# The last stage of a hybrid diffusion step: where its rows wait and how its roots are taken

## What is computed

```python
# x: residual stream after the mixer, (1152, 1024); g2: gate row of the context or of the latents
y = moe(hn2, ...)            # 64 experts, 8 for each token, and a shared one
x = x + g2 * y
def rmsnorm(x, g):
    xf = x.astype(jnp.float32)
    y = xf * lax.rsqrt(jnp.mean(xf * xf, axis=-1, keepdims=True) + EPS)
    return (y * g.astype(jnp.float32)).astype(x.dtype)
y_prompt, y_sample = rmsnorm(xp, norm_final), rmsnorm(xs, norm_final)
```

## Time and profile before

| | us |
|---|---|
| median of 3 runs | 2541.48 (2539.81 to 2545.29) |
| the profiled execution, its whole time | 2549.39 |
| its span, first to last instruction | 2547.6 |
| PE busy in the span | 2070.8 (81%) |
| DVE busy in the span | 1286.5 (50%) |
| ACT / POOL busy in the span | 1012.6 / 720.8 |

### The profile page before, as it was taken

How to read it: one execution, slowest core, us unless ns; L and a number is a source line. 1 busy time by engine, 2 the same in 40 slices (tenths; PEclk the granted TensorE clock), 3 DMA queues, 4 the chain that set the end, 5 groups by cost and what they waited for, 6 DMA issues and landing times. The chain is left out here.

```text
span 2547.6 us, 30701 instructions
## 1 busy us (share of the span) xinstructions
PE 2070.8 (81%) x8155; PEld 1358.9 (53%) x8156; DVE 1286.5 (50%) x2145; ACT 1012.6 (40%) x1458; POOL 720.8 (28%) x648
## 2 busy tenths in 40 slices
PE   2786988599867768970999999999999999999950
PEld 0232433346766754440667666667666666666730
DVE  1546443300254563883555545555555555555647
ACT  0334343100111220110666556566666555555631
POOL 4010010000000000444234544443445444544430
PEclk8788999799978888985999999999999999999975
DMA  9322120110000007222996998877888999997454
GB/s 259 121 74 69 66 100 0 59 45 20 23 3 1 1 7 287 76 75 81 333 297 176 312 344 250 291 206 198 247 247 256 301 305 298 313 293 204 105 148 173
DMA packets 114241, 424.52 MB, mean 167 GB/s; under 512 B 22933, under 2 KB 37269, under 8 KB 89229
## 3 DMA queue, kind: packets, MB, share of 16 engines
q1 hardware_dynamic: 62508, 261.05, 27.8%
q0 software_dynamic: 51376, 162.80, 25.4%
q10 hardware_dynamic: 304, 0.02, 0.0%
HBM read 338.68 MB, written 85.66 MB: 167 GB/s over the span
## 5 line engine op out<-in xcount | busy, mean ns | idle before, releaser
L1715 DVE TENSOR_TENSOR wupl<-w,wuph 128x2048 fp32r<-128x2048 f32 x232 | 521.3, 2289 | 547.3 <-ACT wuph L1681 547.3
L1681 ACT ACTIVATE wuph<-w 128x2048 fp32r x232 | 432.0, 1916 | 38.8 <-SPq L1511 36.5
L1632 PE MATMUL bank<-w,hT 128*128 x912 | 416.0, 599 | 0.9 <-issue 0.3
L1614 PE MATMUL bank<-wuph,xTh 128*128 128x512 f32 x920 | 369.9, 402 | 20.2 <-DVE xTl L1724 19.9
L1614 PE MATMUL bank<-wuph,xTl 128*128 128x512 f32 x920 | 361.4, 393 | 0.0
L1614 PE MATMUL bank<-wupl,xTh 128*128 128x512 f32 x920 | 360.5, 392 | 0.0
L1632 PEld LDWEIGHTS bank<-w,hT 128*128 128x128 f32 x912 | 165.6, 192 | 170.9 <-issue 170.8
L1566 POOL DMA_INDIRECT xg<-hn_scratch,idx_g x118 | 212.1, 1798 | 96.0 <-POOL idx_g L1558 93.1
L1574 POOL DMA_INDIRECT yacc_scratch<-y,idx_s x114 | 185.2, 1624 | 114.8 <-ACT y L1672 67.0
L1671 ACT ACTIVATE y<-bank 128x512 f32<-128x512 f32 x114 | 68.2, 598 | 358.1 <-POOLq L1571 203.7
L1614 PEld LDWEIGHTS bank<-wuph,xTh 128*128 128x128 f32 x920 | 174.2, 189 | 58.7 <-issue 25.1
(11 more groups left out here) (319 smaller groups left out, 2624.7 us busy)
## 6 DMA issues: line engine op xcount, KB each, us to landing
w<-in_exp_w SPq DMA_DIRECT2D x192, 1024.0 KB
wada<-in_w_ada POOLq DMA_DIRECT2D x16, 1024.0 KB, 5.9
wg<-in_w_in SPq DMA_DIRECT2D x12, 1024.0 KB, 5.5
x<-x_scratch SPq DMA_DIRECT2D x18, 512.0 KB, 4.1
wada<-in_w_ada SPq DMA_DIRECT2D x4, 2048.0 KB, 22.5
yacc_scratch<-zero POOLq DMA_DIRECT2D x10, 512.0 KB, 9.1
x_scratch<-x SPq DMA_DIRECT2D x9, 512.0 KB
hn_scratch<-hn SPq DMA_DIRECT2D x9, 512.0 KB
```

Of the source, the lines that this page charges most:

```text
L1614: mm = pe.matmul(b_up[j][:, :], x[:, k, :], w[:, :, k, :], start=(k == 0 and i == 0), stop=(k == KT - 1 and i == 2))
L1632: mm = pe.matmul(b_down[half][:, :], hT[:, i, :], w2[:, bass.ds(slot, 1), i, half * 512:(half + 1) * 512].rearrange("p s n -> p (s n)"), s ...
L1681: act.activation(part13(wup[j][0], half), raw13(e % WSLOT, half), ACT.Copy).then_inc(w_high, 1)
L1715: dve.tensor_tensor(part13(wup[j][1], half), raw13(e % WSLOT, half), part13(wup[j][0], half).bitcast(F32), ALU.subtract).then_inc(w_low, 1)
```

## The change

`w13` is allocated in the program instead of in the expert stage. A view of it, `m.late`, cuts its 12,288 floats into twelve rows of 1024. SP's stream in the expert stage ends with a wait for the last low part, and behind it twelve loads into this view: nine residual tiles, two gate rows and the norm row. The last stage has its nine `y` tiles in nine buffers of their own, which SP requests in a row without a wait; `x`, gates and norm row are read where they lie. Stores free no buffer any more. Roots are taken for three tiles by one set of 16 operations on three columns.

```diff
@@ stage_experts
-        w13 = sb("w13", [P, WSLOT, 2, KT, DE])
+        w13 = m.w13
...
                 down_landed(e, e // WSLOT + 1)
+            sp.wait_ge(w_low, pairs(sp) * 4 + 4)
+            for t in range(NT):
+                sp.dma_start(m.late[:, t, :], m.x2[t * P:(t + 1) * P, :]).then_inc(m.s_late, 16)
+            for s in range(2):
+                sp.dma_start(m.late[:, NT + s, :], m.mods[s:s + 1, 5 * D:6 * D].to_broadcast([P, D])).then_inc(m.s_late, 16)
+            sp.dma_start(m.late[:, NT + 2, :], a["norm_final"].unsqueeze(0).to_broadcast([P, D])).then_inc(m.s_late, 16)
@@ stage_final
+        BATCH = 3
+        x = [m.late[:, t, :] for t in range(NT)]
+        gate, nfrow = [m.late[:, NT + s, :] for s in range(2)], m.late[:, NT + 2, :]
+        y, sq = [sb(f"y6_{t}", [P, D]) for t in range(NT)], sb("sq6", [P, D])
...
-            for s in range(2):
-                sp.dma_start(gate[s][:, :], m.mods[s:s + 1, 5 * D:6 * D].to_broadcast([P, D])).then_inc(s_in, 16)
-            sp.dma_start(nfrow[:, :], a["norm_final"].unsqueeze(0).to_broadcast([P, D])).then_inc(s_in, 16)
             for t in range(NT):
-                if t >= 3:
-                    sp.wait_ge(s_out[t % 3], 16 * (t // 3))
-                sp.dma_start(x[t % 3][:, :], m.x2[t * P:(t + 1) * P, :]).then_inc(s_x[t % 3], 16)
-                sp.dma_start(y[t % 3][:, :], m.yacc[t * P:(t + 1) * P, :]).then_inc(s_x[t % 3], 16)
+                sp.dma_start(y[t][:, :], m.yacc[t * P:(t + 1) * P, :]).then_inc(s_y[t], 16)
...
+            def root(t0):
+                c = slice(t0, t0 + BATCH)
+                dve.wait_ge(x_sq, t0 + BATCH)
+                v = ss[:, c]
                 link(dve.tensor_scalar(v, v, 1.0 / D, EPS, ALU.mult, ALU.add))
-                newton_rsqrt(link, dve, v, rs[:, :], rt[:, :], ri[:, :])
+                newton_rsqrt(link, dve, v, rs[:, c], rt[:, c], ri[:, c])
...
+            dve.wait_ge(m.s_late, 16 * (NT + 3))
+            for t in range(BATCH):
+                add(t)
+            for t0 in range(0, NT, BATCH):
+                if t0 + BATCH < NT:
+                    add(t0 + BATCH)
+                root(t0)
+                for t in range(t0, t0 + BATCH):
+                    dve.scalar_tensor_tensor(x[t], x[t], rs[:, t:t + 1], nfrow, ALU.mult, ALU.mult).then_inc(y_new, 1)
+                    if t > t0 and t + BATCH < NT:
+                        add(t + BATCH)
```

More of the change, by code:

```diff
@@ L1746, in stage_final @@
         sem = lambda name: ctx.enter_context(nc.semaphore(name))
[L1747 to L1752, removed]
+        BATCH = 3
+        x = [m.late[:, t, :] for t in range(NT)]
+        gate, nfrow = [m.late[:, NT + s, :] for s in range(2)], m.late[:, NT + 2, :]
+        y, sq = [sb(f"y6_{t}", [P, D]) for t in range(NT)], sb("sq6", [P, D])
+        ss, rs, rt = sb("ss6", [P, NT]), sb("rs6", [P, NT]), sb("rt6", [P, NT])
+        ri = sb("ri6", [P, NT], I32)
+        s_y, s_out = [sem(f"ld_y6_{t}") for t in range(NT)], sem("st_y")
         dch, x_new, x_sq, y_new = (sem(n) for n in ("dve_chain6", "x3_new", "x3_sq", "y_new"))
@@ L1771, in _ @@
                 dst = o[0][0] if t == 0 else o[1][0, (t - 1) * P:t * P, :]
-                pool.dma_start(dst, x[t % 3][:, :]).then_inc(s_out[t % 3], 16)
-            for j in range(3):
-                pool.wait_ge(s_out[j], 16 * ((NT + 2 - j) // 3))
+                pool.dma_start(dst, x[t]).then_inc(s_out, 16)
+            pool.wait_ge(s_out, 16 * NT)
         @block.scalar
@@ L1781, in _ @@
                     act.wait_ge(x_sq, t)
-                act.activation(sq[:, :], x[t % 3][:, :], ACT.Square, accum_out=ss[:, t:t + 1]).then_inc(x_sq, 1)
+                act.activation(sq[:, :], x[t], ACT.Square, accum_out=ss[:, t:t + 1]).then_inc(x_sq, 1)
         @block.vector
@@ L1788, in add @@
             def add(t):
[L1789 to L1800, removed]
-                link(dve.tensor_scalar(v, v, 1.0 / D, EPS, ALU.mult, ALU.add))
-                newton_rsqrt(link, dve, v, rs[:, :], rt[:, :], ri[:, :])
-                dve.scalar_tensor_tensor(x[t % 3][:, :], x[t % 3][:, :], rs[:, :], nfrow[:, :], ALU.mult, ALU.mult).then_inc(y_new, 1)
+                dve.wait_ge(s_y[t], 16)
+                link(dve.tensor_tensor(y[t][:, :], y[t][:, :], gate[min(t, 1)], ALU.mult))
+                dve.tensor_tensor(x[t], x[t], y[t][:, :], ALU.add).then_inc(x_new, 1)
+            def root(t0):
+                c = slice(t0, t0 + BATCH)
+                dve.wait_ge(x_sq, t0 + BATCH)
+                v = ss[:, c]
+                link(dve.tensor_scalar(v, v, 1.0 / D, EPS, ALU.mult, ALU.add))
+                newton_rsqrt(link, dve, v, rs[:, c], rt[:, c], ri[:, c])
[10 more added lines that the diff above has]
+                        add(t + BATCH)
 INPUTS = ["x_prompt", "x_sample", "c", "state_mlstm_C", "state_mlstm_n", "state_mlstm_m", "state_rglru_h", "c_ctx",
@@ L1858, in program @@
             stage_route(nc, a, m)
+        m.w13 = sb("w13", [P, WSLOT, 2, KT, DE])
+        m.late = m.w13[:, :, :, :, :].rearrange("p s w k n -> p (s w k n)").rearrange("p (t n) -> p t n", n=D)
+        m.s_late = sem("ld_late")
         stage_experts(nc, a, m)
```

## The result

| us | before | changed |
|---|---|---|
| median of 4 runs | 2543.39 (2539.81 to 2546.66) | 2519.22 (2515.06 to 2521.89) |
| the profiled execution, whole / span | 2549.39 / 2547.6 | 2519.7 / 2517.9 |

The ratio is 0.9904, 95% interval 0.9883 to 0.9924: 24.2 us less, inside the stated 2513 to 2527, 2.3 us under the forecast of 2521.5. In a later set, beside other runs of before (2543.61), the same kernel had 2522.87, ratio 0.9921 (0.9903 to 0.9940), 20.7 us less.

A forecast was written before the change was run, and what follows sets the result against it. DVE was taken to bound the last stage; first multiplication at 2479.3, plus 43.7 for DVE's chain, 4.45 and 0.3 for stores, gave 2527.7 against a span of 2547.6. Taken from the median, 2541.48 - 19.9 = 2521.5 us, range 2513 to 2527.

The forecast's parts named there:

- What bounds the stage: Last stage: DVE bounds it, with 65.3 us from first multiplication to last scaling; its dependent small operations take 27.6 us.
- Roots by three: DVE in the last stage: six roots of 3.07 us removed, 18.4 us less; three columns cost nothing more.
- a new wait of 1.3: Ahead of the last root: no addition covers the square of tile 8, so DVE waits 1.3 us.
- Turns of buffers: Last stage: nine y buffers and x in place remove 4.5 us of DVE's waits; loads stay ahead of DVE.
- The first multiplication: Last stage's start: two scatters grow 4 us each, barrier opens at 2475.5, DVE starts at 2479.3, 1.4 us later than before.
- The other bound of this step: First multiplication: late loads, scatters and gather add up, done at 2476.4; with one tile and 1.2 us, 2478.9.
- Rival 1: Seam: engines have room for loads and scatters, barrier stays at 2467.55, first multiplication 8 us earlier: 2513.5; chance 0.10.
- Rival 2: Seam: scatters are served last, each grows 6 us or more, barrier opens at 2478.6: 2524.5; chance 0.20.
- rival 6: Seam: scatters stand behind all late loads, which run at half rate; first multiplication 2502.9, slower at 2545.2; chance 0.02.
- rival 4: Stage end: last three stores go one behind the other at 2.9 us each, end 3.4 us later: 2524.6; chance 0.04.
- rival 5: Seam: SP's wait opens only near the barrier, loads stand behind it, 8.8 us later than forecast: 2530.3; chance 0.04.
- The sum: Whole kernel: the profiled span of 2547.6 us falls to 2527.7, 19.9 us less; from the median, 2521.5.

The follow-up runs named there:

- pairs behind the barrier: Against the changed kernel, all last-stage transfers moved behind the barrier, x and y of each tile in turn; nine buffers, roots by three: 2521.68 us, ratio 0.9916.
- pairs behind the barrier with single roots: The kernel before with nine x and nine y buffers, loads behind the barrier, one root for each tile: 2539.33 us, ratio 0.9983.
- one root: The changed kernel with one root for all nine tiles instead of one for three: 2514.13 us, ratio 0.9886.
- the block behind the barrier: The changed kernel's twelve loads moved as one block behind the barrier, ahead of the nine y: 2533.35 us, ratio 0.9949.

## Why the prediction was right

**What bounds the stage**: right. With single roots and everything else changed, 3.1 of the 24.2 us are left. By the seam, buffers alone give 5.3 us, roots by three another 15.5 (pairs behind the barrier with single roots, 92.1, against the same with roots by three, 76.6), early loads between 0.5 us more and 0.7 less. The first multiplication says the same: with early loads it came at 27.9, 29.1, 28.5 and 27.5 us (changed kernel twice, single roots, one root), with pairs behind the barrier at 28.0, 28.0 and 27.6, and before at 27.7.

**Roots by three**: 18.4 us less forecast, less a new wait of 1.3. Measured chains with the loads early: 60.1 against 43.3, 16.8 us. The wait makes the last addition take 3.70 us to the root's start instead of 2.40, so it is 1.3; a root took 3.15 instead of 3.07 us, 0.2 us over three, the bound that I had set aside. With these, 16.9 are accounted for. In pairs it is 60.2 against 43.7, 16.5 us: there the first three additions are 2.48 to 2.58 us apart, the pace of the loads.

**Turns of buffers**: 4.5 us forecast, 5.1 measured in the chain (65.3 to 60.2). Here a reading was wrong. I took 2.48 us for every `add` from the first one, whose successor had to wait for its tile; the second takes 2482.78 - 2480.37 = 2.41, and the seven others 2.40, in the kernel before already. The 0.6 us that this puts too much on `add` belong to the waits: DVE waited six times, for 0.1 to 1.4 us of idle time each. An instruction that doesn't wait starts 0.08 us before the end of its predecessor (an addition that ends at 2481.63 + 1.23 = 2482.86 is followed by a root at 2482.78), and one that waited has lost that too, which idle time doesn't show. The sum of 65.3 came out all the same, because the 4.5 left over for waits was too small by as much. In the forecast of 43.7 it didn't cancel: 0.7 too much for `add`, 0.2 too little for roots, 43.3 measured.

**The first multiplication**: the mechanism was right, sizes were off a little. Forecast 29.1 from the last low part; measured 27.9 and 29.1. The first scatter grew by 4.0 us (5.0 in the second execution), the second by 3.1 (3.0), where I had taken 4 for both. That the 4 came so near was luck in part. I had a start of 4 us and turns of 2 us beside packets of 8 KB, and took the mean of "both halve" (3) and "only the turns halve" (5). In slices of 0.1 us the first packet of a scatter comes 2.1 us behind its issue when it is alone, and in the first scatter of the changed kernel 5.4 (5.7 in the second execution): 3.3 (3.6) us of growth by the start, beside 4 KB packets, and 0.7 (1.4) by the turns. The loaded scatter of the kernel before, from which I read "over 5" against "1.8" in whole microseconds, has 5.7: 3.6 by the start and 2.4 by the turns. So the start did not shrink with the packets, and the turns did. The second scatter grew less by its start (first packet at 4.8 us) and by its turns (0.4 and 0.3). That the turns cost so little is seen in the packets too: 32 of q0 in a microsecond beside the loads (38 in the next), where it has 34 and then 50 alone. This is before, from 2454 and from 2455:

```profile
q0 software_dynamic: 34, 0.14, 70.5%
...
q0 software_dynamic: 50, 0.20, 102.8%
```

The other bound of this step, the end of all data, had one term wrong: the three broadcasts cost 3.9 and not 5.4 us. With that, loads, scatters and gather add up to 24.7 us from the last low part, and the load queue was empty at about 24. So work does add up, as the windows of the changed kernel say (length, busy of the engines, clock, DMA share, GB/s):

```profile
2442.00:2466.00 24.00, 1.92 (x5) 0.57 (x3) 1.37 (x3) 1.08 (x2) 4.55 (x5) 0.62 0.98 328
2455.00:2460.00 5.00, 0.00 (x0) 0.00 (x0) 0.00 (x0) 0.00 (x0) 1.58 (x1) 0.50 1.03 415
```

The engines were full throughout, at 415 GB/s where only loads moved. Beside a scatter the loads fell to 33 packets a microsecond, from 111 to 119 without one: the loads pay far more than the scatter. Rival 1, which had room for both, failed on this and on the late start. Rival 2 (barrier at 28.4) and the half rate of rival 6 were not seen, nor that of stores in turns (tail 4.97, where rival 4 had 7.85). For rival 5 the block behind the barrier is the trial: its first multiplication was 8.5 us later than the changed kernel's, with 8.8 forecast against my own.

The Trainium skill's page "DMA: Bandwidth & Descriptors" (Queues, rings and completion order), by which an engine goes round between queues by whole packets, is borne out by the 32 packets against 33 of the same microsecond. By that alone the barrier would have opened at 20.0 from the last low part; it opened at 24.5, since the late start recurred.

**The sum**: 19.9 us forecast, 21.3 and 20.1 by the seam, 24.2 and 20.7 by the medians. What the first median has over the seam (2.9 us) is within its interval, which is about 5 us to either side; that it lies ahead of the seam, in the spread of the runs, is not shown.

## What to carry to other kernels

A chain of tiny dependent operations costs by their number (the 16 of a root took 3.07 us on one column, 3.15 on three and 3.28 on nine): batch them over tiles as far as memory allows, and check that the stores behind a larger batch keep its pace (with one root the tail grew from 5.0 to 6.1 us, the chain fell by 6.3). Moving loads ahead of a barrier gains only what the last transfer in front of that barrier doesn't lose by them; where a serial chain of scatters holds the barrier, load earlier, when nothing hangs on a scatter, or behind it in the order of use. And count from an event next to the change: ahead of the seam, two executions of unchanged code differed by over 6 us.

## What the runs showed of the hardware that I had not expected

A scatter that accumulates in DRAM moves its first packets late when another queue is full, and then shares the engines with it, at a loss that is mostly smaller. The times are from its issue, in us; "growth" is over the same scatter alone (7.0 for the first, 7.3 for the second), and "rest" what is left of the growth when the later start is taken off. A longer issue counts as a later start. The first scatter has a gather of POOL behind it in every row, the second has none.

| scatter | first packet | growth | by the start | rest |
|---|---|---|---|---|
| alone (before, both) | 2.1 | 0 | 0 | 0 |
| beside weight packets of 8 KB (before) | 5.7 | 6.0 | 3.6 | 2.4 |
| two tiles asked for before it | 3.0 | 0.8 | 0.9 | -0.1 |
| changed kernel, first (twice) | 5.4, 5.7 | 4.0, 5.0 | 3.3, 3.6 | 0.7, 1.4 |
| changed kernel, second (twice) | 4.8, 4.8 | 3.1, 3.0 | 2.7, 2.7 | 0.4, 0.3 |
| load packets of 8 KB, first | 5.3 | 5.8 | 3.2 | 2.6 |
| one root, first (issue 1.1 us longer) | 6.2 | 5.5 | 4.1 | 1.4 |
| loads asked for behind it (issue 1.1 us longer) | 3.7 | 4.5 | 1.6 | 2.9 |

The start did not depend on whether load packets had 4 or 8 KB, the rest did. A scatter asked for ahead of the loads kept most of its start and lost nearly as much behind it. Which part of the path holds it is open: none of the accounts that I tried covers all rows.
